# A two-layer trunk's feed-forward: two down units, not one, leave their last chunk open until the last activations are ready, and the down tiles rotate over four PSUM banks

## The chip, the cores and the metric

The kernel runs on one core of a Trainium2 chip. The metric is device time in microseconds (us), the median of several executions. Engines are named as in the profile: PE (TensorE matmul), PEld (its weight load), DVE (VectorE), ACT (ScalarE), POOL (GpSimd), SP (SyncE, which issues the weight loads from HBM).

## The reference, cut to what matters

Two layers, each `x += MixerBlock(RMSNorm(x)); x += ConvGLU(RMSNorm(x))`, over 512 prompt tokens and 32 sample tokens, all in float32. The change lies in the second half of each layer:

```python
def conv_glu(h, prev, p):
    u = h @ p['w_up']                         # 1024 -> 5632
    pad = jnp.concatenate([prev, u], axis=1)
    c = p['conv_b'] + p['conv_w'][0] * pad[:, 0:L]
    for j in range(1, CONV_W):                # 3 taps
        c = c + p['conv_w'][j] * pad[:, j:j + L]
    a, g = jnp.split(c, 2, axis=-1)
    return (jax.nn.silu(g) * a) @ p['w_down'], pad[:, -(CONV_W - 1):]   # 2816 -> 1024
```

## The kernel before, in words

Features lie on the 128 partitions, the 544 tokens along the free axis, in two halves of 272 columns. Each float32 product is done as three matmuls on split operands (high x high, high x low, low x high), so every weight unit is prepared on the chip: SP loads it into `raw`, ACT copies it to `whi` (L1007, two halves, rounding to the high part), POOL computes `wlo = raw - whi` (L490, two halves) and then raises `w_ready`. `raw`, `whi` and `wlo` have two slots each, used in turn. ACT may overwrite a slot of `whi` for unit j only when PE has signalled `("end", j - 2)`, the last matmul of unit j - 2; SP may load `raw` for unit j when `w_ready` of unit j - 2 is up.

The 2816 features of the feed-forward are done in two groups, the phases F and G, so that `feed_forward` runs four times in all (two layers, F and G each). One run has 11 up units (`FB = 11`) and then 8 down units (`KC = 8`). An up unit makes one chunk of 128 activations: PE (L602 to L604) writes four tiles, DVE evicts them (L1931 to L1936), ACT and DVE apply the taps, the tanh and the gate (L1364, L1943, L1370, L1950, L1957), ACT writes the high part of the activation (L1375, `ahi`) and DVE the low part (L1963, `alo`). A down unit u makes one chunk of 128 output features: two tiles n = 2u and 2u + 1 (one for each half of the tokens), each a sum over the 11 activation chunks, 33 matmuls (L961 to L963). DVE adds each finished tile into `x` (L1998, L2001, L2003).

The last activation chunk is ready only some time after the last up unit. So the first down unit does its first ten chunks for both halves, waits for `("alo", FB - 1)`, and does the eleventh chunk for both halves; then four small transposes of the conv state rows follow (`conv_rows`, L948), and then the other seven down units, each in one piece.

ACT's part behind the up units: it prepares unit FB + 1, then in a loop `for u in range(1, KC)` it prepares unit FB + u + 1 and, in phase G, does `next_norm(u - 1)` (L1030, L1031) for the norm of the next layer, to which DVE adds `norm_lo` (L1492) and `norm_sum` (L1499). POOL does `lo(phase, j)` in the order of the units. Every engine works its own instruction stream in order; semaphores are the only link between them.

Of the kernel before, what the change touches and what calls it, by code (L numbers as in the profile page):

```python
# [72 lines left out]
FB = FT // 2  # L73
# [161 lines left out]
def program(nc, A, known):  # L235
# [4 lines left out]
    with ctx:  # L240
# [112 lines left out]
        M_BANKS = ("mm0", "mm1", "t", "o")  # L353

        def down_bank(n):
            return ("mm0", "mm1", "t")[(n + 2) % 3]

        def pv(bank, rows, n, off=0):
            return ps[0:rows, BANK[bank] + off:BANK[bank] + off + n]
# [24 lines left out]
        def slot(phase, j):  # L384
            return (j + (phase == "G")) % 2
# [10 lines left out]
        def cache_load(S, e, l, i, hh, name):  # L396

            src = A[f"cache_{name}"][ds(l, 1), 0, :, ds(i * 2 + hh, 1), :].rearrange("a (c p) h d -> p (a c h) d", p=P)
            e.dma_start({"k": kc_n, "v": vc_n}[name][:, :, :], src).then_inc(*S.up(f"cache_{name}{hh}", "in", n=16))
# [10 lines left out]
        def sync_program(S):  # L410
            e = S.e

            def load_unit(phase, j, what):

                e.wait_ge(*S.at("w_ready", k=j - 2))
                n, src = what
                s = slot(phase, j)
                for a in (0, n // 2):
                    e.dma_start(raw[:, s, a:a + n // 2], src[:, a:a + n // 2]).then_inc(*S.up(f"raw{s}", n=16))

            e.dma_start(prob[:, :, 0:4 * DIFF_HD], A["lambdas"]).then_inc(*S.up("lambdas", "in", n=16))
            with S.layers() as l:
                for phase, _ in ORDER:
                    with S.body(phase) as i:
                        us = units(phase, l, i)
                        assert len(us) == UNITS[phase]
                        if phase == "D":

                            for j, what in enumerate(us):
                                load_unit(phase, j, what)  # L430
                                if j == 1:

                                    e.wait_ge(*S.at("o_ready", k=0))
                                    e.wait_ge(*S.at("t_ready", k=0))
                                    e.wait_ge(*S.at("pool_step", k=0))
                                    e.wait_ge(*S.at("act_free_o", k=0))
                                    cache_load(S, e, l, i, 0, "k")
                                    cache_load(S, e, l, i, 0, "v")
                        elif phase == "R":
                            for j, what in enumerate(us):  # L440
                                load_unit(phase, j, what)
                                if j == 1:

                                    e.wait_ge(*S.at("pe_step", k=0))
                                    e.wait_ge(*S.at("dve_step", k=0))
                                    e.wait_ge(*S.at("act_step", k=0))
                                    e.wait_ge(*S.at("act_free_t", k=0))
                                    e.wait_ge(*S.at("dve_free_t", k=0))
                                    e.wait_ge(*S.at("dve_free_o", k=0))
                                    e.wait_ge(*S.at("act_free_o", k=0))  # L450
                                    e.dma_start(decay[:, :, :].rearrange("p h n -> p (h n)"),
                                                         A["tab_decay"][:, ds(i * 2 * SEQ, 2 * SEQ)]).then_inc(
                                                             *S.up("decay_in", "d", n=16))
                                if j in (1, 4):
                                    hh = j // 3

                                    e.wait_ge(*(S.at("dve_free_s1", ("snew", 0)) if hh else S.at("dve_free_s1", k=0)))
                                    e.dma_start(sin[:, :], A["state_ret"][ds(l, 1), 0, ds(i * 2 + hh, 1)]
                                             .rearrange("a h d e -> d (a h e)")).then_inc(*S.up("sin_in", ("s", hh), n=16))
                        else:  # L460
                            for j, what in enumerate(us):
                                load_unit(phase, j, what)

            e.wait_ge(*S.at("w_ready", k=-2))
            for a in (0, UNIT // 2):
                e.dma_start(raw[:, 0, a:a + UNIT // 2], A["w_units"][0, 0, :, a:a + UNIT // 2]).then_inc(*S.up("raw0", n=16))

            for c in range(KC):
                if c < KC - 1:
                    e.wait_ge(*S.at("h_lo", k=c - KC))  # L470
                else:
                    e.wait_ge(*S.at("dve_free_t", k=0))
                e.dma_start(A["y"][c], x[:, c, :]).then_inc(*S.up("y_out", n=16))
            e.wait_ge(*S.at("y_out", k=KC * 16))
            e.wait_ge(*S.at("kv_out", k=0))
            e.wait_ge(*S.at("st_out0", k=0))
            e.wait_ge(*S.at("st_out1", k=0))
            e.wait_ge(*S.at("cs_out", k=0))
            e.wait_ge(*S.at("w_ready", k=0))
# [77 lines left out]
        def pe_program(S):  # L557
            e = S.e
# [13 lines left out]
            def start():  # L572
                free.clear()
# [105 lines left out]
            with S.layers():  # L679
# [130 lines left out]
                with S.body("R"):  # L810
                    start()
                    tile[0] = 0
                    for hh in range(2):
                        u = 3 * hh
# [117 lines left out]
                def feed_forward(phase):  # L932
                    start()
                    for j in range(FB):
                        e.wait_ge(*S.at("w_ready", k=j))
                        for t in range(4):
                            t_tile(j, 1 - t // 2, t % 2, hl1, dve=1 + t % 2, bank=UP_BANKS[j % 2][t], last=(t == 3),
                                   chunk=half_ready if phase == "F" and j == 0 and t < 2 else None)
                            if phase == "F" and j == 0 and t == 0:
                                stats("t")  # L940
                            if phase == "F" and j == 0 and t == 2:
                                spread("mm0", "mm1")

                    def conv_rows():
                        acquire("o", dve=1)
                        e.wait_ge(*S.at("act_step", ("cs", FB - 1)))
                        for q in range(4):
                            ins = e.transpose(pv("o", 2 * FB, P, q * P), cs[:, q, :], ident)  # L948
                        ins.then_inc(*S.up("o_ready", "cs"))

                    def down(u, half, k0, k1):
                        n = 2 * u + half
                        s = slot(phase, FB + u)
                        a, width = half * HALF, HALF + 2 * half
                        out = pv(down_bank(n), P, width)
                        if k0 == 0:
                            acquire(down_bank(n), dve=1 + half)
                        for k in range(k0, k1):
                            wh, wl = (w[:, s, k * P:(k + 1) * P] for w in (whi, wlo))
                            hi, lo = (act[:, k, v, a:a + width] for v in (0, 1))  # L960
                            e.matmul(out, wh, hi, start=(k == 0), stop=False)  # L961
                            e.matmul(out, wh, lo, start=False, stop=False)  # L962
                            ins = e.matmul(out, wl, hi, start=False, stop=(k == FB - 1))  # L963
                        if k1 == FB:
                            ready(ins, ("down", n), *([("end", FB + u)] if half else []))

                    for u in range(KC):
                        e.wait_ge(*S.at("w_ready", k=FB + u))
                        if u == 0:
                            e.wait_ge(*S.at("dve_step", ("alo", FB - 2)))  # L970
                            for half in range(2):
                                down(u, half, 0, FB - 1)
                            e.wait_ge(*S.at("dve_step", ("alo", FB - 1)))
                            for half in range(2):
                                down(u, half, FB - 1, FB)
                            conv_rows()
                        else:
                            for half in range(2):
                                down(u, half, 0, FB)

# [1128 lines left out]
```

## Time and profile before

| | |
|---|---|
| median of 3 runs | 2384.08 us (2383.68, 2384.08, 2388.91) |
| the profiled execution, its own time | 2388.49 us |
| its span, first to last instruction | 2386.6 us |
| mean granted TensorE clock | 0.993 |
| PE busy | 2297.6 us, 96% of the span |
| POOL, DVE, ACT busy | 36%, 47%, 40% |

The span is what the rows below are counted in; 1.9 us lie around it. Start times are us from the start of the span. A matmul row shows the time from its issue until its result is out (0.29 us), while the next one starts about 0.126 us after it, so rows overlap; "idle before" is counted from the end of the row ahead, and what ended it stands behind the arrow.

### The profile page before, as it was taken

Reading aid. Unit: us, or ns where it says so; the run is one execution under the profiler, and the core shown is the slowest. Engines: PE = TensorE matmul, PEld = TensorE weight load, DVE = VectorE, ACT = ScalarE, POOL = GpSimd, SP = SyncE. Lnnn points to the kernel's source line nnn. Section 1 sums busy time; section 2 is a strip of 40 time slices with the busy share of each in tenths; the row PEclk is TensorE's granted clock in tenths of the full one; section 3 lists DMA queues with packets and bytes.
Section 4 is the critical chain, followed back from the end, with each engine's and each line's share of the span. In section 5 each row is a group of like instructions: output and inputs, shape, how many; then the busy total and the mean of one; then the engine's idle time right before and its main releaser. Section 6 shows DMA issues by size and latency. Waiting matters only on the chain.

```text
span 2386.6 us, 50229 instructions
## 1 busy us (share of the span) xinstructions
PE 2297.6 (96%) x17560; PEld 2188.9 (92%) x17560; DVE 1131.4 (47%) x1918; ACT 966.5 (40%) x1829; POOL 851.3 (36%) x380
## 2 busy tenths in 40 slices
PE   5999999999999999999999999999999999999999
PEld 5788889889999999999988898798999999999999
DVE  3644453333545576156344644533345455742663
ACT  3544553333423343244335545533343234422443
POOL 3243232223433343343451342232333443434433
PEclk9999999999999999999999999999999999999999
DMA  4132212121222222322232122122122222223223
GB/s 150 51 102 70 85 60 68 60 90 60 89 72 89 83 88 70 108 89 73 80 99 72 63 83 85 51 83 86 60 72 75 72 89 89 84 75 101 90 67 105
DMA packets 81237, 193.28 MB, mean 81 GB/s; under 512 B 7232, under 2 KB 36000, under 8 KB 81056
## 3 DMA queue, kind: packets, MB, share of 16 engines
q1 hardware_dynamic: 59120, 172.38, 22.0%
q10 hardware_dynamic: 21936, 18.56, 2.4%
q8 instruction: 104, 1.70, 0.3%
q14 instruction: 77, 0.63, 0.1%
HBM read 177.50 MB, written 13.42 MB: 80 GB/s over the span
## 4 chain that ended last, share of the span: by engine, by line
issue 57%; PE 25%; POOL 14%; DVE 2%; ACT 1%; POOLq 0%; DVEq 0%; ACTq 0%
POOL wlo L490 11%; PE ps L602 6%; PE ps L604 6%; PE ps L603 6%; POOL rstd L496 3%; PE ps L961 2%; PE ps L962 2%; PE ps L963 2%; DVE ca L1943 1%; PE ps L641 0%; PE ps L642 0%; PE ps L643 0%; PE ps L669 0%; DVE af L1957 0%; DVE odif L1828 0%
## 5 line engine op out<-in xcount | busy, mean ns | idle before, releaser
L490 POOL TENSOR_TENSOR wlo<-raw,whi 128x1024 fp32r<-128x1024 f32 (+1 forms) x330 | 758.7, 2320 | 1338.4 <-ACT whi L1007 1338.4
L602 PE MATMUL ps<-hl,whi 128*128 128x272 f32 x2496 | 723.6, 290 | 2.4 <-DVE hl L1847 2.4
L604 PE MATMUL ps<-hl,wlo 128*128 128x272 f32 x2496 | 719.6, 288 | 0.0
L603 PE MATMUL ps<-hl,whi 128*128 128x272 f32 x2496 | 718.2, 288 | 0.0
L602 PEld LDWEIGHTS ps<-hl,whi 128*128 128x128 f32 x2496 | 471.6, 189 | 4.3 <-issue 2.8
L604 PEld LDWEIGHTS ps<-hl,wlo 128*128 128x128 f32 x2496 | 470.1, 188 | 0.0
L603 PEld LDWEIGHTS ps<-hl,whi 128*128 128x128 f32 x2496 | 469.7, 188 | 0.0
L641 PE MATMUL ps<-whi,hl 128*128 128x256 f32 x1536 | 446.6, 291 | 11.7 <-ACT rk L1234 10.2
L642 PE MATMUL ps<-wlo,hl 128*128 128x256 f32 x1536 | 438.9, 286 | 0.0
L643 PE MATMUL ps<-whi,hl 128*128 128x256 f32 x1536 | 438.1, 285 | 0.0
L1007 ACT ACTIVATE whi<-raw 128x1024 fp32r<-128x1024 f32 (+1 forms) x330 | 313.2, 996 | 224.0 <-PE ps L963 177.2
L641 PEld LDWEIGHTS ps<-whi,hl 128*128 128x128 f32 x1536 | 296.4, 193 | 18.9 <-ACT rk L1234 11.5
L642 PEld LDWEIGHTS ps<-wlo,hl 128*128 128x128 f32 x1536 | 295.7, 193 | 1.1
L643 PEld LDWEIGHTS ps<-whi,hl 128*128 128x128 f32 x1536 | 296.5, 193 | 0.0
L961 PE MATMUL ps<-act,whi 128*128 128x272 f32 (+1 forms) x704 | 206.1, 293 | 8.1 <-DVE act L1963 7.9
L962 PE MATMUL ps<-act,whi 128*128 128x272 f32 (+1 forms) x704 | 205.8, 292 | 0.0
L963 PE MATMUL ps<-act,wlo 128*128 128x272 f32 (+1 forms) x704 | 204.8, 291 | 0.0
L1943 DVE SCALAR_TENSOR_TENSOR ca<-up,par,ca 128x546 f32<-128x546 f32 x176 | 167.0, 949 | 79.5 <-ACT ca L1364 59.5
L961 PEld LDWEIGHTS ps<-act,whi 128*128 128x128 f32 x704 | 134.6, 191 | 9.9 <-DVE act L1963 8.8
L963 PEld LDWEIGHTS ps<-act,wlo 128*128 128x128 f32 x704 | 134.4, 191 | 0.0
L962 PEld LDWEIGHTS ps<-act,whi 128*128 128x128 f32 x704 | 134.4, 191 | 0.0
L1364 ACT ACTIVATE ca<-up,par 128x546 f32<-128x546 f32 x88 | 74.5, 846 | 66.0 <-DVE up L1936 46.1
(214 smaller groups left out, 2926.5 us busy)
## 6 DMA issues: line engine op xcount, KB each, us to landing
raw<-in_w_units_dram SPq DMA_DIRECT2D x266, 512.0 KB, 4.7
raw<-in_w_down_units_dram SPq DMA_DIRECT2D x64, 352.0 KB, 3.3
out_new_k_prompt_dram<-rawk ACTq DMA_DIRECT2D x8, 512.0 KB, 3.0
out_new_v_prompt_dram<-vd ACTq DMA_DIRECT2D x8, 512.0 KB, 3.0
x<-in_x_dram ACTq DMA_DIRECT2D x8, 272.0 KB, 11.4
out_y_dram<-x SPq DMA_DIRECT2D x8, 272.0 KB, 5.7
kc_n<-in_cache_k_dram SPq DMA_DIRECT2D x8, 256.0 KB, 2.9
vc_n<-in_cache_v_dram SPq DMA_DIRECT2D x8, 256.0 KB, 3.3
```

What stands on the lines that cost most here:

```text
L490: ins = e.tensor_tensor(wlo[:, s, a:b], raw[:, s, a:b], whi[:, s, a:b].bitcast(F32), ALU.subtract)
L602: e.matmul(out, wh, hi, start=(c == 0), stop=False)
L603: e.matmul(out, wh, lo, start=False, stop=False)
L604: ins = e.matmul(out, wl, hi, start=False, stop=(c == KC - 1))
L641: e.matmul(out, hi, wh, start=(c == 0), stop=False)
L642: e.matmul(out, hi, wl, start=False, stop=False)
L643: ins = e.matmul(out, lo, wh, start=False, stop=(c == KC - 1))
L961: e.matmul(out, wh, hi, start=(k == 0), stop=False)
L962: e.matmul(out, wh, lo, start=False, stop=False)
L963: ins = e.matmul(out, wl, hi, start=False, stop=(k == FB - 1))
L1007: e.activation(whi[:, s, a:b], raw[:, s, a:b], ACT.Copy).then_inc(*S.up("hi_ready", ("hi", j, part)))
L1943: e.scalar_tensor_tensor(out=ca[:, s, :], in0=up[:, j % 2, s, v:v + GP], scalar=w(2 + v, j, s), in1=ca[:, s, :], op0=ALU.mult, op1=ALU.add ...
```

## The change

The first two down units, not the first alone, do their first ten chunks before PE waits for the last activations. Then both do their eleventh chunk, and the conv rows follow. Four tiles are open at the same time, so the down tiles use four PSUM banks in rotation (`s0`, `t`, `mm0`, `mm1`) where they used three; the last output store waits for the bank of the last tile, which is now `mm1`.

```diff
         def down_bank(n):
-            return ("mm0", "mm1", "t")[(n + 2) % 3]
+            return ("s0", "t", "mm0", "mm1")[n % 4]
...
-                    e.wait_ge(*S.at("dve_free_t", k=0))
+                    e.wait_ge(*S.at("dve_free_mm1", k=0))
                 e.dma_start(A["y"][c], x[:, c, :]).then_inc(*S.up("y_out", n=16))
...
                         e.wait_ge(*S.at("w_ready", k=FB + u))
                         if u == 0:
                             e.wait_ge(*S.at("dve_step", ("alo", FB - 2)))
+                        if u < 2:
                             for half in range(2):
                                 down(u, half, 0, FB - 1)
+                        if u == 1:
                             e.wait_ge(*S.at("dve_step", ("alo", FB - 1)))
-                            for half in range(2):
-                                down(u, half, FB - 1, FB)
+                            for v in range(2):
+                                for half in range(2):
+                                    down(v, half, FB - 1, FB)
                             conv_rows()
-                        else:
+                        if u > 1:
                             for half in range(2):
                                 down(u, half, 0, FB)
```

## Rows read from the trace of the kernel before

**Rows 1.** The page, part 1: busy us of each engine.

```profile
PE 2297.6 (96%) x17560; PEld 2188.9 (92%) x17560; DVE 1131.4 (47%) x1918; ACT 966.5 (40%) x1829; POOL 851.3 (36%) x380
```

**Rows 2.** The waits of PE: us in total, times, longest.

```profile
PE ps L669 <- DVE rawq L1599: 17.3, 8, 2.2
PE ps L961 <- DVE act L1963: 7.9, 4, 2.0
```

**Rows 3.** Timeline of PE, first feed-forward: start us, us, engine line.

```profile
931.40 0.39 PE L961 MATMUL ps<-act,whi 128*128 128x272 f32 x1
...
938.98 0.29 PE L963 MATMUL ps<-act,wlo 128*128 128x274 f32 x1
941.29 0.40 PE L961 MATMUL ps<-act,whi 128*128 128x272 f32 x1 [2.02 <-DVE act L1963]
...
942.03 0.29 PE L963 MATMUL ps<-act,wlo 128*128 128x274 f32 x1
942.15 0.60 PE L948 MATMUL ps<-small,cs 128*22 128x128 f32 x4
942.51 0.37 PE L961 MATMUL ps<-act,whi 128*128 128x272 f32 x1
```

**Rows 4.** Timelines of DVE and ACT there, same columns.

```profile
923.24 0.44 DVE L1931 TENSOR_TENSOR up<-ps,spread_rstd 128x272 f32<-128x272 f32 x1
...
937.50 2.12 DVE L1957 SCALAR_TENSOR_TENSOR af<-th,ca 128x546 f32<-128x546 f32 x1
939.73 0.66 ACT L1375 ACTIVATE act<-af 128x546 fp32r<-128x546 f32 x1 [3.58 <-DVE af L1957]
940.51 0.73 DVE L1963 TENSOR_TENSOR act<-af,act 128x546 fp32r<-128x546 f32 x1 [0.89 <-ACT act L1375]
942.35 1.47 ACT L1007 ACTIVATE whi<-raw 128x704 fp32r<-128x704 f32 x2 [1.96 <-PE ps L963]
```

**Rows 5.** Timeline of POOL there: the down units FB, FB + 1 and FB + 2.

```profile
922.19 3.70 POOL L490 TENSOR_TENSOR wlo<-raw,whi 128x704 fp32r<-128x704 f32 x2 [6.85 <-ACT whi L1007]
935.06 3.97 POOL L490 TENSOR_TENSOR wlo<-raw,whi 128x704 fp32r<-128x704 f32 x2 [9.17 <-ACT whi L1007]
943.22 3.36 POOL L490 TENSOR_TENSOR wlo<-raw,whi 128x704 fp32r<-128x704 f32 x2 [4.19 <-ACT whi L1007]
```

**Rows 6.** The second feed-forward (phase G): timelines of PE, ACT and POOL.

```profile
1144.30 0.29 PE L963 MATMUL ps<-act,wlo 128*128 128x274 f32 x1
1145.05 0.43 PE L962 MATMUL ps<-act,whi 128*128 128x272 f32 x1
1145.27 0.43 PE L963 MATMUL ps<-act,wlo 128*128 128x272 f32 x1
1144.70 1.47 ACT L1007 ACTIVATE whi<-raw 128x704 fp32r<-128x704 f32 x2 [2.05 <-PE ps L963]
1146.08 0.73 ACT L1030 ACTIVATE hl<-x,par 128x544 fp32r<-128x544 f32 x1
1145.57 3.33 POOL L490 TENSOR_TENSOR wlo<-raw,whi 128x704 fp32r<-128x704 f32 x2 [4.27 <-ACT whi L1007]
```

**Rows 7.** Timeline of DVE in phase G: `norm_lo` alone, and beside POOL.

```profile
1151.41 0.79 DVE L1492 SCALAR_TENSOR_TENSOR hl<-x,par,hl 128x544 fp32r<-128x544 f32 x1
1201.69 1.71 DVE L1492 SCALAR_TENSOR_TENSOR hl<-x,par,hl 128x544 fp32r<-128x544 f32 x1
```

**Rows 8.** Windows behind the four waits: us, busy us (instructions), granted clock, DMA share, GB/s.

```profile
942.00:949.00 7.00, 7.00 (x58) 6.92 (x57) 2.06 (x5) 1.47 (x2) 3.36 (x2) 1.00 0.26 80
1144.00:1151.00 7.00, 7.00 (x46) 6.92 (x45) 1.12 (x4) 2.66 (x4) 3.33 (x2) 0.76 0.22 68
2120.00:2127.00 7.00, 7.00 (x46) 6.92 (x45) 1.02 (x4) 1.47 (x2) 3.34 (x2) 0.76 0.24 74
2324.00:2331.00 7.00, 7.00 (x58) 6.92 (x57) 2.46 (x6) 2.66 (x4) 3.37 (x2) 1.00 0.23 71
```

**Rows 9.** The page, part 6: issues of the down weights, KB each, us to landing.

```profile
raw<-in_w_down_units_dram SPq DMA_DIRECT2D x64, 352.0 KB, 3.3
```

## Prediction

> **What bounds the kernel now.** I read the page first: PE is busy for 96% of the span and no other engine for half of it [rows 1], so an edit counts by what it does to PE's idle time and clock. The list of PE's waits comes second. The wait that the change is about is there: four waits of L961 for L1963, 7.9 us in total, each up to 2.0 us [rows 2]. There is one in each of the four feed-forwards. Third, the timelines of all engines around the first of them. Down unit 0 starts at 931.40, issues its 60 early matmuls until 938.98 (59 steps in 7.58 us, about 0.127 us each), and then stands until 941.29 [rows 3], because `alo` of the last chunk ends at 941.24 [rows 4]. Directly behind the wait come six matmuls, the last at 942.03, four transposes, and unit 1 from 942.51 [rows 3]. Fourth, the granted clock in the 7 us behind each wait: 1.00, 0.76, 0.76, 1.00 [rows 8].
>
> **What the change removes.** With unit 1's first ten chunks, another 60 matmuls or 60 x 0.127 = 7.6 us, ahead of the wait, PE would come to it at 938.98 + 0.13 + 7.6 = 946.7, and `alo` is up at 941.24: 5.4 us of cover. The wait goes in all four. Each costs the idle time of the row plus the part of the preceding matmul's 0.29 us in which nothing was issued (0.29 - 0.13 = 0.16): 7.9 + 4 x 0.16 = **8.5 us saved**. A restarted PE also has a first step of 0.24 in place of 0.13 us; that comes again at any other stop, so it is left out on both sides.
>
> **What it moves: unit 1's start.** Unit 1 now begins 3.4 us earlier, at about 939.11, and needs `w_ready(FB + 1)`. POOL finishes that `wlo` at 935.06 + 3.97 = 939.03 [rows 5]. With the 0.05 us that PE took from the end of L1963 to its restart [rows 3, 4] that is 939.08: just in time. The other three lie alike within 0.1 us. I cost this at 0 to 0.1 us each, 0.1 us in all, but there is no cover left here at all.
>
> **What it moves: the end of unit 0, and this is the price.** `("end", FB)` is raised by the last matmul of unit 0's second tile. ACT waits for it to overwrite that slot with unit FB + 2, POOL waits for ACT, and PE needs the result for unit 2. Before, the end of unit 0 came a whole unit (66 matmuls, 8.4 us) ahead of unit 2. Now only six matmuls of unit 1 and the transposes lie between them. The chain is in the trace as it stands: last matmul of unit 0 issued at T = 942.03 [rows 3], ACT starts at 942.35 and needs 1.47 us [rows 4], POOL runs from 943.22 for 3.36 us until 946.58 [rows 5]. That is T + 4.55. In phase G it is 1144.30 to 1145.57 + 3.33 = 1148.90, T + 4.60 [rows 6]. PE is through with its own work at T + 6 x 0.127 + 0.48 (942.03 to 942.51, the transposes' step) = T + 1.24. The new wait, restart included, is 4.55 + 0.05 - 1.24 = 3.36 us in F and 3.41 us in G: 2 x 3.36 + 2 x 3.41 = **13.5 us added**. What is queued behind it on PE: all of unit 2, and through it the rest of the run, since PE is the bound.
>
> **What rides on the same chain.** In phase G ACT does `next_norm(0)` right behind the two copies (L1030 at 1146.08, that is T + 1.78 [rows 6]). DVE follows with `norm_lo(0)` at about T + 2.55; before, it came much later, at 1151.41, beside an idle POOL, and took 0.79 us [rows 7]. Now it falls into POOL's two instructions (T + 1.27 to T + 4.60). The same instruction beside POOL took 1.71 us [rows 7], and a POOL pair beside DVE's L1943 and L1957 took 3.97 instead of 3.36 us [rows 5]. So POOL is held for 0 to 0.8 us in each G; I take the row's difference, 0.6, twice: **1.2 us**. The Trainium skill, page "SBUF — State Buffer", section on the two sides of SBUF, says that the port pair shared by VectorE and GpSimd is an exclusive lock, which a VectorE operation with two SBUF inputs takes against a GpSimd operation that reads SBUF, and the other blocks in full. By that rule POOL would lose the whole 0.79 us, 1.6 us for both; the trace agrees in kind (1.71 against 0.79). The evictions of tiles 0 to 3, which now come in one burst within 3 us, read one operand from PSUM. The eviction at 923.24 took 0.44 us in the middle of POOL's pair at 922.19 [rows 4, 5], so DVE is not held; that pair took 0.34 us more than the bare 3.36, beside it and other DVE work. I take nothing for them, and keep 0.3 us for each of the four as the upper end.
>
> **The rest at nothing, with its cover.** Banks: tiles 0 to 3 go to `s0`, `t`, `mm0`, `mm1`, whose last up tiles are those of units 9 and 10, the latest of them evicted at 923.24 + 0.44 [rows 4], before unit 0 starts; tile 4 needs `s0` back, evicted during the new wait. Without a fourth bank the fourth open tile could not exist, so it is a condition, not a gain: no wait for a bank is in the list before. `raw` for unit FB + 4 is loaded when `w_ready(FB + 2)` is up, T + 4.6, and lands 3.3 us later [rows 9]; ACT wants it only after the end of unit 2, T + 13. If that cover were gone it would cost its excess over 5 us. Unit FB + 3: its copies follow on ACT at once, POOL is done at about T + 4.6 + 3.4 = T + 8 (G: T + 9), PE wants it at T + 13. So the chain catches up within one unit and the wait does not repeat. The conv rows' copy and stores move by some us under PE's work.
>
> **The clock.** Of the four waits of 2.0 us, two were followed by a window at clock 0.76 [rows 8]: matmuls stepping by 0.22 instead of 0.13 us (1145.05 to 1145.27) [rows 6], the lower level, 1.2 GHz. In both windows 46 matmuls were issued in place of 58, so 12 x 0.127 = 1.5 us each, 3.0 us in the execution. The new waits are 3.4 to 4.0 us, longer than the 2.0 and 2.2 us of the rows [rows 2], so I expect that all four are followed by such a stretch, but that in about half of them part of it passes while PE still stands, costing less: 4 x 1.3 = 5.2. Net **+2.2 us**, with bounds of -3.0 (none falls) and +3.0 (4 x 1.5).
>
> **The sum.** -8.5 + 0.1 + 13.5 + 1.2 + 2.2 = **+8.5 us** against the profiled execution's 2388.49: 2397.0. The median before is 4.4 us lower, with two of three runs near 2384 and one near the profile's. I read the difference as fewer stretches at the lower clock, in which case such a run pays up to 5.2 rather than 2.2 for the clock: 2384.08 + 8.5 = 2392.6 to 2384.08 + 11.5 = 2395.6. I take **2395**.
>
> **Rivals.**
>
> *The wait goes and nothing takes its place (faster).* For this `w_ready(FB + 2)` would have to be up by T + 1.24. ACT's and POOL's rows alone need over 4 us behind the end of unit 0, so either the `whi` slot is free earlier than I read it or the chain is shorter by 3.3 us. It decides from a chain under 3.4 us, at which the new wait equals the old one. It would give -8.5 - 3.0 = 2388.49 - 11.5 = 2377, or 2373 to 2376 on the median. Chance 0.05.
>
> *The new wait is little worse than the old (no change).* The weight chain runs as in the rows, no hold on POOL, and the clock loses nothing more, or less than before because the slow stretch passes while PE stands: -8.5 + 13.5 = +5.0, less up to 3.0. On 2384.08 that is 2386 to 2389, and its lower part lies within 0.2%. Chance 0.17.
>
> *As forecast*: new waits of 3.3 to 4.2 us, a stretch at the lower clock behind most of them, +6 to +13 us, 2390 to 2397. Chance 0.60.
>
> *Two waits in series (slower still).* `w_ready(FB + 1)` has no cover, so if it is late by a few tenths, and each long wait leaves the clock low for longer than the short ones did, up to two such stretches each, the clock term becomes 4 x 3.0 and the sum 2384.08 + 6.3 + 12 = 2402. For it: the margin of 0.03 us. Against it: the stretches behind the waits of 2.0 us all ended inside 7 us [rows 8]. Chance 0.18.
>
> **Numbers.** A difference of 0.2%, 4.8 us, is about what a measurement of this kernel can tell from no change. Range 2387.5 to 2401.5: the forecast, the upper part of "no change" and most of the last case; the likeliest one's own range is 2390 to 2397. Slower by over 0.2%: 0.60 + 0.18 + a small part of "no change" = 0.80. Within: 0.15. Faster: 0.05.
>
> **What would show it.** In the profile after: L961 <- L1963 gone from PE's waits; in its place four waits of L961 for POOL's L490, 3.0 to 4.0 us each (idle from the matmul's or transposes' end, so about 0.2 us less than my figures), the two in G longer by half a microsecond; about 4.55 us from the last matmul of unit 0 to the end of L490; L1492 of the first chunk in G at 1.2 to 1.7 us; clock near 0.76 in the 7 us behind most of them; no wait on a PSUM bank. The prediction is wrong if the wait for L490 is under 2 us, if the clock stays at 1.00 behind it, or if PE loses time at the start of unit 1.

## The result, and the profile after

| | before | after |
|---|---|---|
| median of 8 runs each | 2384.47 us (2383.68 to 2390.35) | 2393.48 us (2392.0 to 2394.94) |
| profiled execution, span | 2386.6 us | 2393.1 us |
| mean granted TensorE clock | 0.993 | 0.991 |

The ratio is 1.0032, 95% interval 1.0022 to 1.0043: 0.3% slower, 9.0 us by the medians. Line numbers behind line 975 are 3 higher than before (L1007 is now L1010, L1492 is L1495, L1963 is L1966); in the kernels of the experiments they move by up to 11.

The waits of PE in the changed kernel, which answer to [rows 2]:

```profile
PE ps L616 <- DVE acc L1502: 27.7, 1, 27.7
PE ps L669 <- DVE rawq L1602: 17.2, 8, 2.2
PE ps L961 <- POOL wlo L490: 13.7, 4, 3.7
PE ps L641 <- ACT rk L1237: 10.2, 6, 2.2
```

The four waits for the activations (7.9 us) are gone, and four waits for POOL's weights (13.7 us) stand in their place. Now the first feed-forward on PE, as in [rows 3]:

```profile
937.95 0.29 PE L963 MATMUL ps<-act,wlo 128*128 128x274 f32 x1
938.12 0.39 PE L961 MATMUL ps<-act,whi 128*128 128x272 f32 x1
...
946.46 0.29 PE L963 MATMUL ps<-act,wlo 128*128 128x274 f32 x1
...
947.22 0.29 PE L963 MATMUL ps<-act,wlo 128*128 128x274 f32 x1
947.35 0.60 PE L948 MATMUL ps<-small,cs 128*22 128x128 f32 x4
...
951.09 0.39 PE L961 MATMUL ps<-act,whi 128*128 128x272 f32 x1 [3.15 <-POOL wlo L490]
```

PE goes from unit 0 into unit 1 (938.12) with a step of 0.17 in place of 0.13 us (0.17 and 0.19 us in the other three feed-forwards). Unit 0 ends at T = 946.46, the last matmul of unit 1 is issued at 947.22, the transposes follow, and unit 2 starts at 951.09, T + 4.63. The same stretch on ACT, POOL and DVE, which answers to [rows 4, 5]:

```profile
946.79 2.83 ACT L1010 ACTIVATE whi<-raw 128x704 fp32r<-128x704 f32 x4 [7.44 <-PE ps L963]
947.66 6.61 POOL L490 TENSOR_TENSOR wlo<-raw,whi 128x704 fp32r<-128x704 f32 x4 [9.67 <-ACT whi L1010]
938.69 0.66 ACT L1378 ACTIVATE act<-af 128x546 fp32r<-128x546 f32 x1 [3.59 <-DVE af L1960]
939.47 0.73 DVE L1966 TENSOR_TENSOR act<-af,act 128x546 fp32r<-128x546 f32 x1 [0.89 <-ACT act L1378]
```

The last activations are ready at 940.20, 5.6 us before PE's first matmul on them, at 945.83. ACT had been idle for 7.44 us until the end of unit 0 let it go; then it copies units FB + 2 and FB + 3 in one piece, and POOL works 6.61 us behind it. Unit FB + 3 is ready long before PE is through with unit 2, so the wait does not repeat. Phase G, which answers to [rows 6, 7]:

```profile
1151.53 0.29 PE L963 MATMUL ps<-act,wlo 128*128 128x274 f32 x1
...
1156.72 0.39 PE L961 MATMUL ps<-act,whi 128*128 128x272 f32 x1 [3.71 <-POOL wlo L490]
1152.80 3.79 POOL L490 TENSOR_TENSOR wlo<-raw,whi 128x704 fp32r<-128x704 f32 x2 [9.77 <-ACT whi L1010]
1154.27 0.79 DVE L1495 SCALAR_TENSOR_TENSOR hl<-x,par,hl 128x544 fp32r<-128x544 f32 x1 [1.26 <-ACT hl L1033]
```

Here the distance is 5.19 us: POOL's pair took 3.79 instead of 3.33 us [rows 6] with `norm_lo` inside it. Last, windows of 15 us that begin near the end of unit 1 (up to 2.2 us ahead of it) and hold the whole wait, one for each feed-forward; the column behind the fifth busy time is the granted clock:

```profile
945.10:960.10 15.00, 11.85 (x82) 11.51 (x82) 3.00 (x8) 2.83 (x4) 6.61 (x4) 0.89 0.31 100
1152.20:1167.20 15.00, 11.29 (x77) 10.95 (x77) 4.97 (x11) 5.25 (x9) 7.10 (x4) 0.89 0.32 101
2126.40:2141.40 15.00, 11.85 (x82) 11.51 (x81) 3.00 (x8) 2.83 (x4) 6.60 (x4) 0.89 0.31 100
2333.50:2348.50 15.00, 11.29 (x78) 10.95 (x77) 4.99 (x11) 5.27 (x9) 7.09 (x4) 0.89 0.32 101
```

Before, 2 of the 4 waits had a stretch at the lower clock behind them [rows 8]; now all four have one. Counted over the whole of the two profiles, the kernel before has ten such stretches and the changed one twelve (one that is twice as long counted as two): eight of each lie elsewhere, so the difference is in these four places.

### The profile page after: what moved, and what is told of

It is laid out like the page before. It is cut to its first block, busy times and chain, and to the rows that moved or that the text cites. A ratio compares the mean times of both kernels' runs of the same rounds, so it can differ in the third digit from the quotient of the medians.

```text
span 2393.1 us, 50167 instructions
## 1 busy us (share of the span) xinstructions
PE 2300.9 (96%) x17560; PEld 2192.2 (92%) x17560; DVE 1129.6 (47%) x1918; ACT 967.1 (40%) x1829; POOL 852.2 (36%) x380
## 4 chain that ended last, share of the span: by engine, by line
issue 77%; POOL 20%; PE 2%; POOLq 1%; ACT 0%; DVE 0%; ACTq 0%
POOL wlo L490 16%; POOL rstd L496 3%; PE ps L961 1%; PE ps L962 1%; PE ps L963 1%; POOLq L489 0%; POOL rsr L539 0%; POOLq L226 0%; POOL rs L502 0%; POOLq L165 0%; POOL qz L523 0%; POOL odif L519 0%; POOLq L495 0%; ACT xs L1041 0%; POOL rawq L517 0%
## 5 line engine op out<-in xcount | busy, mean ns | idle before, releaser
L641 PE MATMUL ps<-whi,hl 128*128 128x256 f32 x1536 | 446.1, 290 | 10.2 <-ACT rk L1237 10.2
L1010 ACT ACTIVATE whi<-raw 128x1024 fp32r<-128x1024 f32 (+1 forms) x330 | 312.9, 996 | 231.9 <-PE ps L963 185.3
L641 PEld LDWEIGHTS ps<-whi,hl 128*128 128x128 f32 x1536 | 296.1, 193 | 17.2 <-ACT rk L1237 11.4
L961 PE MATMUL ps<-act,whi 128*128 128x272 f32 (+1 forms) x704 | 207.4, 295 | 13.9 <-POOL wlo L490 13.7
L961 PEld LDWEIGHTS ps<-act,whi 128*128 128x128 f32 x704 | 136.1, 193 | 16.1 <-issue 15.9
```

Source lines behind the costliest of these rows:

```text
L641: e.matmul(out, hi, wh, start=(c == 0), stop=False)
L1010: e.activation(whi[:, s, a:b], raw[:, s, a:b], ACT.Copy).then_inc(*S.up("hi_ready", ("hi", j, part)))
```

## Experiments

The runs of one kernel scatter by some us (the kernel before, over all its runs, from 2382.5 to 2390.4). Medians here are good to 1 or 2 us: banks_only and banks_again are one and the same kernel and came out 1.6 and 0.1 us above the kernel before. The waits in the profile tell more than the times do.

### The banks alone: banks_only, banks_again

The order of before, with the change's two lines on the banks.

```diff
-            return ("mm0", "mm1", "t")[(n + 2) % 3]
+            return ("s0", "t", "mm0", "mm1")[n % 4]
...
-                    e.wait_ge(*S.at("dve_free_t", k=0))
+                    e.wait_ge(*S.at("dve_free_mm1", k=0))
```

> The order of before with the four banks of the change. Theory W (the price is the weight chain behind the late end of unit 0): nothing moves, 2384 us, ratio 1.000 within 0.001, the four waits of L961 for the low part of the last activations stay at 7.9 us. Rival B (the rotation with s0, next to the up tiles' banks, costs the time): the loss of the change, up to 9 us, appears here.

Measured: 2386.13 against 2384.53 us, ratio 1.0007 (0.9998 to 1.0016). PE's waits are the old ones:

```profile
PE ps L961 <- DVE act L1963: 7.9, 4, 2.0
```

That is not the loss of the change, but 1.6 us was left open, so the same kernel ran again.

> banks_only once more. If its 1.6 us were the spread of the clock's stretches (two of three runs of before lie near 2384, one near 2389), the median is now within 1 us of before's on either side; if they belong to the banks, it is again 1.5 us or more above.

Measured: 2384.42 against 2384.33 us, ratio 1.0000 (0.9991 to 1.0009). The banks cost nothing that can be measured, and rival B, that the rotation is the loss, falls.

### A shorter piece ahead of the wait: one_half_ahead

Three banks. Eight chunks of unit 1's first tile cover the wait, then unit 0 is ended, then unit 1.

```diff
                         if u == 0:
                             e.wait_ge(*S.at("dve_step", ("alo", FB - 2)))
                             for half in range(2):
                                 down(u, half, 0, FB - 1)
+                        elif u == 1:
+                            down(u, 0, 0, 8)
                             e.wait_ge(*S.at("dve_step", ("alo", FB - 1)))
                             for half in range(2):
-                                down(u, half, FB - 1, FB)
+                                down(0, half, FB - 1, FB)
                             conv_rows()
+                            down(u, 0, 8, FB)
+                            down(u, 1, 0, FB)
                         else:
```

> Three banks as before; only 8 chunks of unit 1's first tile (24 matmuls, 3.0 us) are put ahead of the wait, then unit 0 is ended at once and unit 1 is finished. Theory W: the wait of 2.0 us is covered and unit 0 still ends a whole 42 matmuls (5.3 us) ahead of unit 2, more than the 4.55 us of the weight chain less the transposes, so neither wait is there: 8.5 us of idle PE and the slow clock behind it are saved, 2373 to 2376 us, no wait of L961 over 0.3 us. Rival C (unit 1 has no cover at its start, or PE is held at the same point by something else): gain under 4 us, a wait of L961 for L490 at the start of unit 1.

Measured: 2373.23 against 2384.53 us, ratio 0.9956 (0.9942 to 0.9969), faster than both kernels. L961 is not in PE's list of waits at all. POOL's work for unit FB + 2 (first line) lies wholly beside PE's, and the clock is at its upper level (the two windows):

```profile
943.32 3.37 POOL L490 TENSOR_TENSOR wlo<-raw,whi 128x704 fp32r<-128x704 f32 x2 [5.09 <-ACT whi L1011]
941.60:956.60 15.00, 15.00 (x121) 14.92 (x120) 3.00 (x8) 2.95 (x4) 6.73 (x4) 1.00 0.33 105
1143.00:1158.00 15.00, 15.00 (x121) 15.00 (x120) 5.20 (x12) 6.17 (x10) 7.51 (x5) 1.00 0.31 101
```

So covering the activations was sound; what cost the time was how late unit 0 ended.

### The distance between the end of unit 0 and unit 2: eight_chunks, five_chunks

The change with 8, and with 5, in place of 10 chunks of unit 1 ahead of the wait (the second edit is the same with 5).

```diff
                             for half in range(2):
-                                down(u, half, 0, FB - 1)
+                                down(u, half, 0, FB - 1 if u == 0 else 8)
...
                                 for half in range(2):
-                                    down(v, half, FB - 1, FB)
+                                    down(v, half, FB - 1 if v == 0 else 8, FB)
```

> The change, but unit 1 does eight chunks of each tile ahead of the wait, not ten, so 18 matmuls and not 6 lie between the end of unit 0 and unit 2. Theory W: the new wait shrinks by 12 x 0.127 = 1.5 us in each of four places, from the 3.1 and 3.7 us of the changed kernel to 1.6 and 2.2 us (7.6 us in all); the total is 6 us or more under the changed kernel, 2384 to 2388. Rival B or D (it is the number of open tiles, not the distance): time and wait as in the changed kernel, 2393.

Measured: 2383.45 against 2384.53 us, ratio 0.9994 (0.9985 to 1.0003), 10.0 us under the changed kernel and half a microsecond under the range that was expected. Its waits, 1.6 us in each F and 2.2 in each G:

```profile
PE ps L961 <- POOL wlo L490: 7.7, 4, 2.2
```

The waits are those expected, 6.0 us less than in the changed kernel. The expectation left out the clock: only one of the four waits, the last, has a stretch at the lower clock behind it, not four, and three stretches are about 4.5 us.

> As eight_chunks with five chunks of each of unit 1's tiles ahead of the wait: 30 matmuls, 3.8 us, cover the wait of 2.2 us for the activations, and 36 matmuls (4.6 us) and the transposes lie behind the end of unit 0, against a chain of 4.6 us in F and 5.1 us in G. Theory W: neither wait is left in F, at most 0.1 us in G; the time is that of one_half_ahead, 2373 to 2376 us, though four banks and four open tiles are used as in the change. Rival D (four open tiles cost something of their own): over 2378 us.

Measured: 2374.85 against 2384.47 us, ratio 0.9952 (0.9939 to 0.9966), and no wait of L961. With 6, 18 and 36 matmuls behind the end of unit 0 PE waits 13.7, 7.7 and 0 us: one matmul more takes 0.125 us off each wait ((13.7 - 7.7) / 4 / 12), which is the step of a matmul. Four open tiles and four banks are in all three, so rival D, that four open tiles cost something of their own, falls too.

### The chain made shorter: after_half_lo

The changed kernel, but the second half of the low part of the weights is left out for unit FB + 2 alone (stale values stand there).

```diff
+            def lo_first_half(phase, j):
+                n = prep_len(phase, j)
+                s = slot(phase, j)
+                for part in (0, 1):
+                    e.wait_ge(*S.at("hi_ready", k=2 * j - 1 + part))
+                e.tensor_tensor(wlo[:, s, 0:n // 2], raw[:, s, 0:n // 2], whi[:, s, 0:n // 2].bitcast(F32), ALU.subtract).then_inc(
+                    *S.up("w_ready", ("lo", j)))
...
-                        lo("F", j)
+                        (lo_first_half if j == FB + 2 else lo)("F", j)
...
-                        lo("G", j)
+                        (lo_first_half if j == FB + 2 else lo)("G", j)
```

> The change, with the second half of the low part left out for the weights of unit FB + 2 alone (both copies are waited for, then one POOL instruction of 1.7 us and not two). Theory W: PE waits for this chain and nothing else, so w_ready of that unit comes at about 1.9 + 1.7 = 3.65 us behind the end of unit 0 instead of 4.6 (F) and 5.1 (G): the waits fall from 3.1 to 2.2 us in F and from 3.7 to 2.2 us in G, 8.8 us in all in place of 13.7, and the time by 5 us or a little more, to 2387 to 2389 us. Rival (the load of raw or another engine is the last link): the waits stay near 3.1 and 3.7 us.

Measured: 2385.73 against 2384.47 us, ratio 1.0000 (0.9991 to 1.0009). The waits (the matmul's line is 8 higher here):

```profile
PE ps L969 <- POOL wlo L498: 8.9, 4, 2.3
```

8.9 us where 8.8 was expected: PE follows POOL's last instruction to a tenth. The time fell by 7.8 us, to 1.3 us under the expected range; 4.8 us of it is idle time, and the rest is in keeping with the clock, since behind these waits of 2.2 us only two of four windows of 15 us show it at 0.89, not four.

### What holds POOL in phase G: norm_later

The changed kernel, but in phase G ACT does `next_norm(0)` behind its copies for unit FB + 3, not behind those for unit FB + 2.

```diff
-                        if phase == "G":
-                            next_norm(u - 1, None)
+                        if phase == "G" and u > 1:
+                            if u == 2:
+                                next_norm(0, None)
+                            next_norm(u - 1, None)
```

> The change, but ScalarE does the next norm's first chunk in phase G one place later, behind its copies for unit FB + 3, so that VectorE's norm_lo(0) falls behind or into the second half of POOL's work for unit FB + 2 and can no longer hold it. Theory (the shared port: norm_lo holds POOL): the two waits in G fall from 3.7 to 3.1 to 3.2 us, as in F, the total from 13.7 to 12.5 us; the time falls by about 1 us, less than the runs can tell. Rival (G is slower for another reason: ScalarE's start or a DMA): they stay at 3.7 us.

Measured: 2392.35 against 2384.47 us, ratio 1.0031 (1.0021 to 1.0042).

```profile
PE ps L961 <- POOL wlo L490: 12.8, 4, 3.2
```

All four waits are now 3.15 to 3.23 us: the additional 0.5 us of G came from `norm_lo` beside POOL. The time does not tell this from the changed kernel, as expected. `norm_lo(0)` now starts inside POOL's second instruction for unit FB + 2 (1152.59, 1.67 us) and is held itself, at 1.06 instead of 0.79 us:

```profile
1153.78 1.06 DVE L1497 SCALAR_TENSOR_TENSOR hl<-x,par,hl 128x544 fp32r<-128x544 f32 x1 [2.62 <-ACT hl L1033]
```

The hold on POOL has not gone away; it has moved. POOL's next instruction, the first for unit FB + 3 (1154.22), takes 2.17 instead of 1.67 us. PE does not wait for that unit, so it costs nothing.

### The clock by itself: after_filled, before_filled

Matmuls that nobody reads, into the free bank `s1`, keep PE busy in the wait.

```diff
+                    def filler(n):
+                        acquire("s1")
+                        for k in range(n):
+                            e.matmul(pv("s1", P, HALF), act[:, 0, 0, 0:P], act[:, 1, 0, 0:HALF], start=True, stop=True)
...
                     for u in range(KC):
+                        if u == 2:
+                            filler(26)
                         e.wait_ge(*S.at("w_ready", k=FB + u))
```

In before_filled it is `filler(16)` ahead of the wait for `("alo", FB - 1)` in the kernel before.

> The change with 26 matmuls that nobody reads (272 columns each, 3.3 us, into the free bank s1) ahead of the wait for unit 2's weights. The wait is the same, only PE is busy in it. Theory: what is left of the change's loss beyond the idle time is the lower clock behind the waits, 4 x 1.3 = 5.2 us, so this runs at about 2388 to 2390 us, with clock 1.00 in the 7 us behind each wait. Rival: if the clock is not part of it, the time stays at 2393 us or grows with the added work.

Measured: 2389.87 against 2384.53 us, ratio 1.0020 (1.0011 to 1.0030). PE's own gap in G is down to 0.6 us, and the clock stays at its upper level in all four places. In F PE does not stand at all, and the fillers overshoot a little: in the first one unit 2 starts 3.96 us behind the last matmul of unit 1 (3.87 in the changed kernel). The first two windows:

```profile
946.50:961.50 15.00, 15.00 (x120) 14.71 (x119) 3.12 (x9) 3.05 (x5) 6.71 (x4) 1.00 0.31 101
1152.20:1167.20 15.00, 14.45 (x115) 14.16 (x115) 5.21 (x12) 6.72 (x11) 8.00 (x5) 1.00 0.32 101
```

> The kernel before with 16 matmuls that nobody reads (2.0 us, into the free bank s1) ahead of the wait for the last activations. The wait's time is still spent. Theory: behind a wait of 2.0 us the clock falls in about two of four places, 1.5 us each, so this gains 0 to 6 us, about 3: 2381 to 2384 us, no 3.4 us stretch at the lower clock behind any of the four waits. Rival (stretches at the lower clock come by themselves and not from the wait): they stay, and the time is 2384.5 or more.

Measured: 2382.72 against 2384.47 us, ratio 0.9990 (0.9981 to 0.9999), no slow stretch behind the four places. By the medians the clock behind the waits is worth 1.8 us in the kernel before and 3.6 us in the changed one. The 3.6 us are clear of the scatter: the runs of after_filled (2386.76 to 2391.93) all lie under those of the changed kernel (2392.0 to 2394.94). The 1.8 us only just are, the interval of the ratio ending at 0.9999. The profiles give more for the changed kernel: its span less PE's first wait is 2393.1 - 27.7 = 2365.4 us, that of after_filled 2388.7 - 29.4 = 2359.3, 6.1 us less, which is four stretches at 1.5 us.

### The better order, with three and with four banks: one_half_again, one_half_four_banks

The first is the kernel of one_half_ahead as it is; the second has the two bank lines of the change besides.

> one_half_ahead once more, beside its twin with four banks: 2373 to 2375 us.

> one_half_ahead with the four banks of the change. banks_only left open whether the rotation costs up to 0.16% (3.8 us). If it costs nothing, this is within 1 us of one_half_again, no wait of L961. If the rotation cost what banks_only's median showed, this is 1.6 us or more slower.

Measured, against 2384.33 us: 2372.95 us, ratio 0.9947 (0.9933 to 0.9960), and 2373.64 us, ratio 0.9952 (0.9938 to 0.9966). Neither has a wait of L961. The 0.7 us between them is under what these runs tell apart. The fourth bank is neither a cost nor a gain here.

## Why the prediction held, step by step

**What is removed, 8.5 us: right.** L961 <- L1966 is out of the list. one_half_ahead shows the size: -11.3 us, against 8.5 us of idle time and a clock term of 1.8 us (before_filled) to 3.0 us (two stretches at 1.5 us in the profile).

**Unit 1's start, 0.1 us: right.** 0.17 to 0.19 in place of 0.13 us, 0.2 us in all. It had no cover and needed none. The half of the rival "two waits in series" that hung on it falls.

**The end of unit 0, 13.5 us: right.** T + 4.63 was measured where T + 4.60 was worked out. From the last matmul of unit 1 to unit 2 it is 951.09 - 947.22 = 3.87 us, less the transposes' 0.48: 3.39 us, against 3.36. That the chain is the cause is shown by both its ends: more matmuls behind the end of unit 0 (eight_chunks, five_chunks) and less work for POOL (after_half_lo) shorten the wait by their own length.

**The hold on POOL, 1.2 us: near in size, wrong in what would show it.** G's distance is 5.19 us, 0.56 more than F's, and norm_later takes it away. POOL's pair was held for 0.46 us (3.79 less 3.33), 0.9 us for both G, where 1.2 was put down. I had expected L1495 itself to be lengthened to 1.2 to 1.7 us. It took 0.79: it started at 1154.27, 0.17 us before POOL's second instruction at 1154.44, so POOL was the one that was held, at 2.15 instead of 1.68 us. The Trainium skill, page "SBUF — State Buffer", section on the two sides of SBUF, says that of a VectorE operation with two SBUF inputs and a GpSimd operation that reads SBUF, the one that starts first gets the shared port pair for its whole instruction, and the other blocks. The trace agrees in kind. The hold was not the instruction's whole 0.79 us, since they overlapped in part only, by 0.62 us, and it was shorter than the overlap by 0.1 to 0.2 us each time: 0.47 us here, 0.50 of 0.62 for POOL's next unit in norm_later, 0.27 of 0.48 for DVE there, and nothing of 0.21 for DVE beside the end of POOL's first instruction here. The evictions from PSUM, put at nothing, cost POOL nothing: in F, beside them, its two units took 6.61 us, 3.3 each.

**The clock, +2.2 us: right in sign; its parts were off.** All four waits were followed by a stretch at 1.2 GHz, as forecast (granted clock 0.51 from 952.60 to 956.00). None of them passed while PE stood, as I had assumed for half of them: they lay behind PE's restart (the first matmuls at 951.09 to 951.81 still step by 0.12 us), and in the 7 us from 951.30, 1157.00, 2133.00 and 2338.30 on PE issued 45 matmuls each, against 57 in one_half_ahead. So they cost their full 1.5 us each, and the net in the profile is 6.0 - 3.0 = +3.0. The fillers give 3.6 - 1.8 = +1.8 between medians. The forecast lies between.

**The sum.** In the profile: idle time 2 x 3.39 + 2 x (1156.72 - 1152.29 - 0.48 = 3.95) = 14.7, less 8.5: +6.2; clock +3.0; together +9.2. The spans differ by 6.5. The rest lies elsewhere and is not the change's: PE's first wait, on the loads at the start, is 27.7 us and not 28.8, and one wait of the kernel before is missing after:

```profile
PE ps L616 <- DVE acc L1499: 28.8, 1, 28.8
...
PE ps L641 <- ACT rawq L1080: 1.5, 1, 1.5
```

9.2 - 1.1 - 1.5 = 6.6 us. That these 2.6 us are chance is borne out by the other traces: PE's first wait is between 26.3 and 29.4 us over all thirteen, in no order of the kernels, and banks_only and banks_again, one kernel, have 28.5 and 26.6 us for it and 0.9 and nothing for L641 <- L1080. The executions say the same: the profiled one lay 4.0 us over the median before (2388.49 against 2384.47) and 1.5 us over it after (2394.94 against 2393.48), and the medians differ by 9.0 us.

The forecast of 2395 was 1.5 us high. The rows gave +8.5 us, and 2384.47 + 8.5 = 2393.0 would have been 0.5 us from what was measured. What raised it was my reading of the 4.4 us between profile and median as fewer stretches at the lower clock in the median run. The record speaks against that. The profiled execution had a mean clock of 0.993, as had 36 of the 65 runs of the kernel before that were made beside the experiments, and these took 2383.1 to 2387.3 us. The traces of banks_only and banks_again, which have the order of before, show two slow stretches behind their four waits as well, and banks_again took 2383.27 us with them. So a typical run before most likely paid for about two stretches too, and the clock term is the net of the profiles; which runs had how many is not on record.

**The rivals.** "Nothing takes its place" wanted a chain under 3.4 us; it is 4.6. "Little worse than the old" is what eight_chunks makes of it, not the change. "Two waits in series" did not occur: no second wait, and a clock of 0.89 in 15 us around each wait, which is one stretch at the lower clock, not two.

## What to carry to other kernels

Work put ahead of a wait covers it only as far as it is longer than the wait; what goes beyond delays whatever the waiting work releases. Here a wait of 2.2 us was covered with 7.6 us of matmuls, and with that the end of the unit, which gives back the weight slot, came 7.6 us closer to its next use, while the refill needs 4.6 us. So before moving work across a wait, list what the delayed instruction signals, and how far behind it the next user of that signal will stand: 3.0 us ahead and 42 matmuls behind were both enough, and gave 11 us.

## What the runs showed of the hardware

Whether a stop of PE is followed by a stretch at 1.2 GHz went by its length, and not with certainty:

| stop of PE | kernels | followed by a stretch |
|---|---|---|
| 1.9 to 2.0 us | before, banks_only, banks_again | 6 of 12 |
| 1.6 and 2.2 us | eight_chunks | 1 of 4, a stop of 2.2 us |
| 2.2 to 2.3 us | after_half_lo | 2 of 4 |
| 3.1 to 3.7 us | the changed kernel, norm_later | 8 of 8 |
| filled with matmuls, at most 0.6 us idle | before_filled, after_filled | 0 of 8 |

The same stop thus does not always have the same price: about 1.5 us or nothing. That is part of the scatter of this kernel's runs, with the stretches that lie elsewhere. Of the 65 runs of the kernel before, the eight with a mean clock of 0.991 took 2387.3 to 2389.3 us, the twenty with 0.994 took 2382.5 to 2385.2. Another part is PE's first wait, 26.3 to 29.4 us.
